# Two-layer hybrid encoder trunk: the squares of h for the RMS norms added in pairs on GpSimd ahead of the product with ones, and one weight's split moved behind the squares

## What is computed

```python
def rms_norm(x, g):
    xf = x.astype(jnp.float32)
    y = xf * lax.rsqrt(jnp.mean(xf * xf, axis=-1, keepdims=True) + RMS_EPS)
    return (y * g.astype(jnp.float32)).astype(x.dtype)

h = h + 0.5 * rms_norm(swiglu(rms_norm(h, g[0]), ffn_w_gu[i, 0], ffn_w_down[i, 0]), g[1])
h = h + rms_norm(mixer(rms_norm(h, g[2])), g[3])
h = h + 0.5 * rms_norm(swiglu(rms_norm(h, g[4]), ffn_w_gu[i, 1], ffn_w_down[i, 1]), g[5])
```

## Time and profile before

| | us |
|---|---|
| median of 3 runs (2283.71 to 2288.39) | 2287.49 |
| the profiled execution's own time | 2284.82 |
| its span in the profile | 2283.0 |
| TensorE busy in the span | 2202.5 (96%) |
| VectorE busy | 1092.4 (48%) |
| ScalarE busy | 804.8 (35%) |
| GpSimd busy | 467.9 (20%) |
| mean granted TensorE clock | 0.975 of full speed |
| share of the last-ending chain: TensorE, VectorE, ScalarE, GpSimd | 85%, 10%, 3%, 1% |

### The profile page before, as it was taken

The page is one execution under the profiler, slowest core; times in us unless marked ns, Lnnn a source line. Parts: engine busy times, 40 slices in busy tenths (PEclk is TensorE's granted clock), DMA queues, the critical chain, the costliest instruction groups (busy, mean ns, idle before and its releaser), DMA issues.

```text
span 2283.0 us, 51042 instructions
## 1 busy us (share of the span) xinstructions
PE 2202.5 (96%) x22812; PEld 1867.3 (82%) x22812; DVE 1092.4 (48%) x1562; ACT 804.8 (35%) x1388; POOL 467.9 (20%) x595
## 2 busy tenths in 40 slices
PE   7999998999899999999999999999998999999997
PEld 6888887877699965788888888888886667888886
DVE  5433325767566555843332563333274537433323
ACT  4333313565233343533331343332142424433320
POOL 2111112420223223511110221110151204111102
PEclk9999999999999999999999999999999779999999
DMA  4323321320000012232232122232132012323311
GB/s 160 130 93 105 123 88 38 131 68 20 13 4 4 4 57 94 80 124 99 100 127 88 50 100 102 103 121 102 56 92 84 1 37 75 111 93 118 127 52 38
DMA packets 29099, 183.43 MB, mean 80 GB/s; under 512 B 3232, under 2 KB 8160, under 8 KB 9936
## 3 DMA queue, kind: packets, MB, share of 16 engines
q1 hardware_dynamic: 28032, 178.79, 22.3%
q0 software_dynamic: 848, 1.37, 0.3%
HBM read 174.31 MB, written 4.30 MB: 78 GB/s over the span
## 4 chain that ended last, share of the span: by engine, by line
PE 85%; DVE 10%; ACT 3%; POOL 1%; issue 1%; DMA 0%; SPq 0%; DVEq 0%; POOLq 0%; ACTq 0%
PE psum L289 67%; PE psum L1634 6%; DVE arena L355 2%; DVE arena L403 1%; PE psum L1625 1%; PE psum L381 1%; PE psum L2527 1%; PE psum L2526 1%; PE psum L2513 1%; PE psum L1658 1%; DVE arena L393 1%; DVE arena L331 1%; DVE split L264 1%; PE psum L2357 1%; DVE h L360 1%
## 5 line engine op out<-in xcount | busy, mean ns | idle before, releaser
L289 PE MATMUL psum<-x,split 128*128 128x256 f16 (+1 forms) x5568 | 638.7, 276 | 7.1 <-POOL x L422 5.5
L289 PEld LDWEIGHTS psum<-x,split 128*128 128x128 f16 x5568 | 542.9, 98 | 99.3 <-issue 15.1
L289 PE MATMUL psum<-x,split_more 128*128 128x256 f16 (+1 forms) x2496 | 287.1, 276 | 2.5 <-DVE x L2625 1.5
L289 PE MATMUL psum<-x,arena 128*128 128x256 f16 (+2 forms) x2448 | 281.1, 276 | 7.6 <-DVE arena L657 6.8
L725 POOL TENSOR_TENSOR arena<-arena 128x256 f16<-128x256 f32 (+1 forms) x176 | 120.4, 684 | 797.6 <-ACT arena L574 797.6
L289 PEld LDWEIGHTS psum<-x,split_more 128*128 128x128 f16 x2496 | 244.6, 98 | 39.6 <-issue 1.9
L289 PEld LDWEIGHTS psum<-x,arena 128*128 128x128 f16 (+1 forms) x2448 | 240.2, 98 | 43.1 <-DVE arena L264 7.3
L264 DVE SCALAR_TENSOR_TENSOR split<-stage,split 128x2048 f16<-128x2048 f32 (+1 forms) x77 | 189.9, 2467 | 157.4 <-ACT split L258 157.4
L289 PE MATMUL psum<-arena,split 128*128 128x256 f16 (+1 forms) x2304 | 261.6, 275 | 0.0
L289 PEld LDWEIGHTS psum<-arena,split 128*128 128x128 f16 x2304 | 225.4, 98 | 35.0 <-issue 2.5
L652 DVE SCALAR_TENSOR_TENSOR arena<-psum,arena 128x256 f32<-128x256 f32 (+1 forms) x176 | 75.5, 429 | 311.1 <-ACT arena L568 306.4
(11 more groups left out here) (220 smaller groups left out, 2601.6 us busy)
## 6 DMA issues: line engine op xcount, KB each, us to landing
stage<-in_w_gu SPq DMA_DIRECT2D x88, 1024.0 KB, 4.9
stage<-in_w_down SPq DMA_DIRECT2D x32, 1408.0 KB, 6.1
stage<-in_w_rkv SPq DMA_DIRECT2D x12, 1024.0 KB, 5.0
stage<-in_w_out SPq DMA_DIRECT2D x4, 1024.0 KB, 4.7
stage<-in_w_q SPq DMA_DIRECT2D x4, 1024.0 KB, 4.8
stage<-in_w_o SPq DMA_DIRECT2D x4, 1024.0 KB, 5.7
h_spill<-h SPq DMA_DIRECT2D x1, 2112.0 KB, 12.0
out<-h SPq DMA_DIRECT2D x8, 256.0 KB, 2.1
```

The lines of the kernel that those rows point to most:

```text
L289: last = pe.matmul(o, wt(wp, k), xs(xp, k), start=(k == 0 and wp == 0 and xp == 0), stop=(k == tiles - 1 and wp == 1))
```

## The change

`add_h` is followed by three additions on GpSimd in every turn with a pre norm: `sq` tile 0 += tile 1, 2 += 3, 4 += 5, each waiting for the second square of its pair. In the opening turn, which has no `add_h`, they stand in GpSimd's queue ahead of the rests of each half. `pre_total` then has five products, for the `sq` tiles 0, 2, 4, 6 and 7, in place of eight; the first three wait for the pair, the last two for ScalarE's square. At the end of the FFNs (not of the mixers) ScalarE's `split_hi` of the next block's weight 1 stands behind the squares of tiles 5 to 7, where it stood ahead of them.

```diff
@@ -177,6 +177,7 @@
+        h_pairs = by_half("square_pairs")
@@ -364,6 +365,17 @@
                 pool.tensor_tensor(h[:, k, a:a + n], h[:, k, a:a + n], tmp[:, k % 4, 0:n], ALU.add).then_inc(h_new[s], 1)
+            if T.pre_gain is not None:
+                pair_squares(pool, T, s)
+
+        SQ_PAIRS = 3
+
+        def pair_squares(pool, T, s):
+            n = T.spans[s][1]
+            for j in range(SQ_PAIRS):
+                pool.wait_ge(h_sq[s], KT * T.pre + 2 * j + 2)
+                pool.tensor_tensor(sq[:, 2 * j, 0:n], sq[:, 2 * j, 0:n], sq[:, 2 * j + 1, 0:n], ALU.add).then_inc(
+                    h_pairs[s], 1)
@@ -376,8 +388,11 @@
         def pre_total(pe, T, s):
             n = T.spans[s][1]
-            for k in range(KT):
-                pe.wait_ge(h_sq[s], KT * T.pre + k + 1)
+            for k in [*range(0, 2 * SQ_PAIRS, 2), *range(2 * SQ_PAIRS, KT)]:
+                if k < 2 * SQ_PAIRS:
+                    pe.wait_ge(h_pairs[s], SQ_PAIRS * T.pre + k // 2 + 1)
+                else:
+                    pe.wait_ge(h_sq[s], KT * T.pre + k + 1)
                 last = pe.matmul(psum[:, 6 + s, 0:n], c("ones"), sq[:, k, 0:n], start=(k == 0), stop=(k == KT - 1))
@@ -635,8 +650,8 @@
                 square_h(e, T_out, 0, 0, 5)
                 squares(5, 1)
+                square_h(e, T_out, 0, 5, KT)
                 split_hi(e, T_out.jobs[1])
-                square_h(e, T_out, 0, 5, KT)
                 pre_root(e, T_out, 0)
@@ -726,7 +741,9 @@
                 if opening:
+                    pair_squares(e, T, 0)
                     T.how.rest(e, T, 0)
+                    pair_squares(e, T, 1)
                     rest(0, 0)
```

## The result

The changed kernel takes 2290.05 us (median of 12 runs, 2287.03 to 2294.95) against 2285.79 for the kernel before over 12 runs: ratio 1.0023, 95% interval 1.0013 to 1.0033, so 3.0 to 7.5 us slower. The forecast was +3.3 us, inside the interval; 2290.8 was predicted for the median. The profiled execution has a span of 2290.0, 7.0 longer than before, more than the medians moved. One of the six executions of experiment 7's kernel took 3693.55 us at a granted clock of 0.56 and is left out of its ratio.

A forecast was written before the change was run, and what follows sets the result against it. TensorE, busy 96%, was taken to bound the kernel, but VectorE to lead at the mixers' ends. Place-by-place terms summed to +3.3 us, which against 2287.49 gave 2290.8 us; range 2280 to 2297.

The forecast's parts named there:

- Prices: At each place, three fewer float32 products save TensorE 1.30 us; each GpSimd pair beside VectorE's tail costs VectorE 0.44.
- rival 2: Beside VectorE's work, at ten places: each pair holds VectorE for its whole 0.73 us; 2298.6 us, chance 0.12.
- FFN ends: Half 0, later split plus pairs delay `pre_inverse`: +0.60 us before RWKV, +1.68 before the third FFN, +1.68 at attention.
- Mixer ends, half 0: Two places: all three pairs lie beside VectorE's tail and VectorE leads, +1.30 us each.
- Half 1: Second half of the later turns: -0.43 us before RWKV, -0.10 third FFN, -0.40 attention, -1.0 last FFN.
- 0 in the second FFN: Second half after a mixer: TensorE is freed 1.3 us later, then the total is 1.30 shorter, net 0.
- rival (3): At TensorE's longer waits: the clock falls, each drop adding 2.7 us, or 1.7 for ten passes; two give 2295, chance 0.15.
- all waits but one start well below 3.7: Argument against slowing through the clock: TensorE's waits, except one, begin far shorter than 3.7 us.
- the 3.7: TensorE's wait in us past which the clock was taken to fall; 3.71 preceded the low stretch in the last FFN.
- rival 1: At all places: the pairs cost VectorE nothing; -7.5 us, giving 2280 us, chance 0.15.
- rival 4: At all places: TensorE sets the end and the change gains the whole 15.5 us; 2272 us, chance 0.06.
- rival 5: Whole kernel: the edit changes nothing that counts, covers being larger than read; 2287.5 us, chance 0.05.

The follow-up runs named there:

- experiment 7: Kernel before with three pairs in the opening turn, three late pairs at half 1 after each mixer, two at other half 1s: 2280.8 us, ratio 0.9973.
- experiment 3: Changed kernel with each of GpSimd's three additions replaced by a memset, which reads nothing: 2281.61 us, ratio 0.9987 to the kernel before.
- experiment 1: Kernel before with only the split of weight 1 moved behind the squares at the three FFN ends, no pairs: 2285.71 us, ratio 1.0002.
- experiment 2: Changed kernel with the split of weight 1 back ahead of the squares: 2304.14 us, ratio 1.0078 to the kernel before.
- experiment 4: Changed kernel with eight products in place of five behind the pairs: 2297.59 us, ratio 1.0053 to the kernel before.
- experiment 5: Kernel before with three pairs and five products in the opening turn alone, both halves: 2284.92 us, ratio 0.9991.
- experiment 6: Kernel before with pairs in the opening turn and, after VectorE's split, at half 1 behind each mixer: 2281.83 us, ratio 0.9982.
- experiment 8: Kernel before with two pairs and six products at all twelve places, split of weight 1 in its old place: 2292.24 us, ratio 1.0026.

## Why the prediction was right, point by point

- **Prices.** Ten passes at full clock last 2.32 and sixteen 3.62: 1.30 less, as worked out. A pair pushes VectorE by 0.44 to 0.50: the tail ahead of the third FFN moved by 0.95 for two pairs (0.88), the end of the RWKV mixer by 1.47 for three (1.32). So the price was a tenth low.
- **The rule that the pair holds VectorE for its whole length** (rival 2): the additions last 0.9 and push by 0.44 to 0.50, and the FFN ends and mixer ends came out within 0.2 of the sum that goes by 0.44. Out, as to the length of the hold; that there is one was shown by experiment 3.
- **FFN ends**: +0.49, +1.58, +1.57 for +0.60, +1.68, +1.68. Experiment 1 shows the move's own share as 0.64 where I had 0.80, experiment 2 what it prevents. One step failed: I said that `post_total` (L320, now L321) would wait over 2 us for the sums. It waits 0.39, for TensorE came later itself: the 84 matmuls between the total and x took 10.97, and 9.33 before, behind the wait that had grown to 2.26. In experiment 1, where these matmuls took 9.33 as before, it does wait 2.26. The end is the same, since VectorE sets it; that the fall of the clock fell into time that was lost anyway is luck.
- **Mixer ends, half 0**: +1.47 and +1.35 for +1.30; with eight products or five, as experiment 4 shows.
- **Half 1**: -0.30 for -0.43, +0.20 for -0.10, -0.14 for -0.40, -0.79 for -1.0: each entry a little worse than worked out. In the third FFN the last tile of the input sets the end, as I reasoned, for the +0.20 is the same with eight products (experiment 4); `pre_inverse` was 1.46 late and not 1.3, and with 0.20 left over the spare time was 1.26 and not 1.4.
- **The step that was wrong** is "0 in the second FFN". It measured +1.33. The delay of 1.30 was there: TensorE's wait ended 1.28 later. The saving was not: behind the wait of 4.40 the three matmuls ahead of the total took 0.3 more than before and the ten passes 3.38, where sixteen had taken 3.62. The cause is that of rival (3), at the place that it names, and the 1.06 that the ten passes took beyond the 2.32 of full clock is within its 1.7. I could have seen it: the wait in the kernel before was 3.11, so "all waits but one start well below 3.7" was a wrong reading, and 3.11 + 1.30 is past the 3.7 at which I let the clock decide. In the ten profiles this wait was 3.11 or 3.12 six times (before, experiments 1, 3, 5, 6, 7), and the total ran at the half clock behind it in two of them (3 and 6). It was 4.01 to 4.57 four times (the changed kernel, experiments 2, 4, 8), and the clock fell in all four. Experiments 6 and 7 have the same code there and show what one fall is worth: ten passes took 4.01 in one and 2.48 in the other, and the ledger has +0.40 and -1.12.
- **Slower through the clock** (rival 3) is therefore not out but small. Its sign, more stretches of low granted clock, did show: three new ones outside the mixers, one at the beginning of the second FFN and one each at the ends of the second and the third. Two of the three cost nothing, as VectorE led there.
- **Free pairs** (rival 1): out by L361. **TensorE leads everywhere** (rival 4) and **nothing counts** (rival 5): out by experiments 4 and 7.
- The opening's -2.06 for -1.30 was probably no error of the step: 1.27 of it is the products by the means of nine profiles, each group spread over about 1.
- **Luck.** In the one profile the opening's surplus of -0.76 takes back more than half of the +1.33 that I had at 0. The medians, which average over such placing, moved by 4.3 and not 3.3. The mechanism was right; the sum matches better than its terms do.

What stays open: the +3.35 in attention. The instructions are the same and the granted clock differs. From `pre_inverse` of half 1 to the next `post_inverse` this profile grew by 1.9; with five products there experiments 2 and 3 grew by 0.2 and 0.9, with six experiments 7 and 8 by 0.3 and 0.5, and the kernels with eight by -2.1 to +0.1. The spread within a group (1.7 and 2.2) is as large as the distance between their means (1.6), and no run sets the clock alone, so I can't say how much is chance.

## What to carry to other kernels

An engine with 20% of busy time isn't free: GpSimd's additions beside VectorE instructions with two SBUF inputs cost VectorE 0.44 to 0.50 each, and where VectorE leads, saved matmuls buy nothing. The same additions put where VectorE works from PSUM did not lengthen its instructions. That, and no pairs at all at half 0 of the turns, turned +0.23% into -0.27%. Before work is taken from a busy engine, ask place by place which engine comes last there; a table of places with a sign for each is the forecast.

## What I had not expected of the hardware

Stretches at the half clock stand behind waits of TensorE much shorter than the 3.7 that I had taken from the earlier trace rows: behind 2.26 at two FFN ends of the changed kernel, 2.75 (experiment 8), 4.40 and 5.84, and behind 3.1 in two profiles and not in four others. In that case the same ten passes took 2.48 and 4.01 us. That the wait brings the fall is argued from this order, as no run sets the wait alone. A saving of matmuls ahead of a wait makes the wait longer, and seems able to lose by the clock what it gains in work: experiment 8 came out 6 us above its forecast, and 4.9 of that stand at the three places named there in its profile.
